# A routing table's buffers move under another expert weight slot, and two weight loads move with them

## What is computed

```python
x = x + merged(rms_norm(x)) @ w_out          # mixer: spatial gating + RG-LRU, sigmoid-gated
xf = rms_norm(x, norm2)
g_idx = argmax of 4 groups;  e_idx = top 2 of the group's 8 experts
h = silu(xf @ w_gate[e]) * (xf @ w_up[e])    # 32 experts: [1024, 256] each
x = x + sum over the 2 experts of gate * (h @ w_down[e])
y = rms_norm(x, norm_f)
```

## The kernel before

| bytes | slot | what stands there earlier |
|---|---|---|
| 0 to 48 | wslot00, wslot01 | v; free long before stage O |
| 48 to 72 | wslot20 | xh, xl |
| 72 to 96 | wslot21 | 72 to 80: wh2, wl2, used until the last unit of stage O; 80 to 97: zT, free before stage O |
| 98 to 122 | wslot10 | mh, ml, used until the last unit of stage O |
| 122 to 146 | wslot11 | ml until 130, raw from 130 to 146; from 138 on the routing tables (R_T), while they are used |

## Time and profile before

### The profile page before, as it was taken

The page is one execution under the profiler, slowest core; times in us unless marked ns, Lnnn a source line. Parts: engine busy times, 40 slices in busy tenths (PEclk is TensorE's granted clock), DMA queues, the critical chain, the costliest instruction groups (busy, mean ns, idle before and its releaser), DMA issues.

```text
span 646.4 us, 8845 instructions
## 1 busy us (share of the span) xinstructions
PE 597.8 (92%) x2860; PEld 357.3 (55%) x2860; DVE 322.9 (50%) x672; ACT 229.1 (35%) x393; POOL 53.1 (8%) x126
## 2 busy tenths in 40 slices
PE   6899999999999999999999978999999988997794
PEld 3676697877777777777568633433333333332321
DVE  4834698867767677685666764111111112111058
ACT  5414335474664746647264311111111111110124
POOL 1200001000000000000000021112121221111000
PEclk9899999999999999999999978999999999999995
DMA  8421316831222322221597489999999999999993
GB/s 306 157 95 66 114 49 228 342 104 67 73 73 97 97 74 73 73 98 55 198 396 310 179 338 369 418 421 420 419 420 420 421 419 421 418 420 420 414 317 138
DMA packets 33448, 160.61 MB, mean 248 GB/s; under 512 B 6320, under 2 KB 6704, under 8 KB 21008
## 3 DMA queue, kind: packets, MB, share of 16 engines
q1 hardware_dynamic: 27808, 149.52, 58.8%
q0 software_dynamic: 5472, 10.63, 4.5%
q10 hardware_dynamic: 144, 0.15, 0.1%
HBM read 155.01 MB, written 14.17 MB: 262 GB/s over the span
## 4 chain that ended last, share of the span: by engine, by line
PE 60%; SPq 13%; DVE 10%; DMA 10%; ACT 3%; issue 3%; ACTq 0%; DVEq 0%; POOLq 0%
PE ps L1486 12%; PE ps L1488 12%; PE ps L1487 12%; SPq L537 11%; PE ps L1829 8%; PE ps L1855 5%; DMA wslot<-in_wmoe 5%; PE ps L1605 2%; PE ps L1637 2%; DMA gy<-ytok 2%; DVE wl L908 1%; DMA ytok<-yo,idx 1%; PE ps L1691 1%; DMA raw<-in_wmix 1%; PE ps L1589 1%
## 5 line engine op out<-in xcount | busy, mean ns | idle before, releaser
L1829 PE MATMUL ps<-wslot,xgT 128*64 128x512 f32 x528 | 121.7, 594 | 11.4 <-DMA wslot<-in_wmoe 10.0
L699 ACT ACTIVATE wh<-raw 128x1024 fp32r<-128x1024 f32 x56 | 59.1, 1058 | 151.4 <-PE ps L1488 135.1
L1486 PE MATMUL ps<-xh,wh 128*128 128x512 f32 x256 | 102.5, 400 | 0.0
L1488 PE MATMUL ps<-xl,wh 128*128 128x512 f32 x256 | 100.0, 390 | 0.0
L1487 PE MATMUL ps<-xh,wl 128*128 128x512 f32 x256 | 99.9, 390 | 0.0
L908 DVE TENSOR_TENSOR wl<-raw,wh 128x1024 fp32r<-128x1024 f32 x56 | 68.5, 1223 | 46.7 <-ACT wh L699 45.6
L1829 PEld LDWEIGHTS ps<-wslot,xgT 128*64 128x64 f32 x528 | 40.0, 137 | 88.3 <-issue 86.5
L1855 PE MATMUL ps<-wslot,hT 128*64 128x512 f32 x264 | 63.8, 613 | 8.4 <-ACT hT L869 7.6
L1402 DVE SCALAR_TENSOR_TENSOR hm<-ps,rt,hs 128x256 f32<-128x256 f32 x12 | 5.8, 483 | 122.3 <-ACT hs L867 122.3
L1486 PEld LDWEIGHTS ps<-xh,wh 128*128 128x128 f32 x256 | 48.1, 188 | 16.1 <-issue 6.7
L1488 PEld LDWEIGHTS ps<-xl,wh 128*128 128x128 f32 x256 | 48.1, 188 | 10.6
(11 more groups left out here) (331 smaller groups left out, 796.0 us busy)
## 6 DMA issues: line engine op xcount, KB each, us to landing
wslot<-in_wmoe SPq DMA_DIRECT2D x97, 1024.0 KB, 21.4
raw<-in_wmix SPq DMA_DIRECT2D x56, 512.0 KB, 4.1
gy<-ytok SPq DMA_DIRECT2D x8, 512.0 KB, 8.7
xt<-in_x SPq DMA_DIRECT2D x4, 512.0 KB, 7.0
x<-in_x SPq DMA_DIRECT2D x4, 512.0 KB, 4.7
xnd<-x SPq DMA_DIRECT2D x4, 512.0 KB, 7.8
wslot<-in_wmoe SPq DMA_DIRECT2D x4, 512.0 KB, 27.3
out_y<-yf SPq DMA_DIRECT2D x4, 512.0 KB, 2.7
```

What stands on the lines that cost most here:

```text
L699: a.activation(WH[hslot], raw[:, slot, :, :].rearrange("p k c -> p (k c)"), ACT.Copy).then_inc(hi_ready, 1)
L1486: pe.matmul(out, sh, mh_, start=start, stop=False)
L1488: return pe.matmul(out, sh, ml_, start=False, stop=stop)
L1829: l = pe.matmul(ps[CAP * s:CAP * s + CAP, 2, :], xgT[:, c, CAP * s:CAP * s + CAP], wslot[q][s][:, c * 512:(c + 1) * 512], start=c == 0, st ...
```

## The change

1. The routing tables (R_T) move from 138 KB (under wslot11, part 2) to 80 KB (under wslot21, parts 1 and 2), into the memory of zT, which is free by then. `junk2` moves to 88 KB, into the same slot.
2. With that the gap of 1 KB that junk2 needed behind zT is closed: R_M, R_W, R_V, yf, wslot10, wslot11 and the small tensors lie 1 KB lower. rkx, chk, bx, posx and dgs get memory of their own.
3. The order on SP follows. Parts 1 and 2 of expert 5 are no longer issued in stage O. All three parts of expert 5 now stand behind the wait for `rt_mm`, and part 2 of expert 3 stands ahead of that wait. The stores of GROUP_A's rows (`row_out`) stand in the loop, at its last turn, which is the same place.

PE, DVE, ACT and POOL execute the same instructions in the same order as before.

```diff
-             for q, first in enumerate((0, 98, 48))]
+             for q, first in enumerate((0, 97, 48))]
...
-    R_V = 162 * K
+    R_V = 161 * K
...
-    R_M = 98 * K
+    R_M = 97 * K
...
-    R_W = 130 * K
+    R_W = 129 * K
...
-    R_T = R_W + 8 * K
+    R_T = 80 * K
...
-    junk2 = at("junk2", 96 * K, [P, 512])
-    yf = at("yf", 122 * K, [P, TILES, D])
+    junk2 = at("junk2", R_T + 8 * K, [P, 512])
+    yf = at("yf", 121 * K, [P, TILES, D])
...
-    (rkx, chk, bx, posx) = [at(n, upper_at + 256 + i * 64, [P, T2]) for i, n in enumerate(("rkx", "chk", "bx", "posx"))]
+    (rkx, chk, bx, posx) = [small(n, [P, T2]) for n in ("rkx", "chk", "bx", "posx")]
...
-    dgs = at("dgs", upper_at, [S, 2, S])
+    dgs = small("dgs", [S, 2, S])
...
             for n in range(48, STEPS):
                 step_in(n)
-                if n % 2 and n < 54:
-                    expert_part(2, 0, 4, (n - 49) // 2)
-            expert_part(2, 1, 5, 1)
-            expert_part(2, 1, 5, 2)
-            for p in range(*GROUP_A):
-                row_out(p, 4 + p)
+                if n % 2:
+                    if n < 54:
+                        expert_part(2, 0, 4, (n - 49) // 2)
+                    else:
+                        for p in range(*GROUP_A):
+                            row_out(p, 4 + p)
             row_out(3, 9)
             row_out(4, 10)
             e.wait_ge(unit_done, STEPS)
...
             e.wait_ge(xg_in, 16)
             expert_part(1, 1, 3, 1)
+            expert_part(1, 1, 3, 2)
             e.wait_ge(rt_mm, 1)
-            expert_part(1, 1, 3, 2)
-            expert_part(2, 1, 5, 0)
+            expert(2, 1, 5)
```

More of the change, by code:

```diff
@@ L173, in build @@
     hT = at("hT", R_E + 14 * K, [P, 2, P])
-    top = [182 * K]
+    top = [181 * K]
     def small(name, shape, dt=F32):
@@ L187, in build @@
     ones = small("ones", [P, P], F32)
-    upper_at = top[0]
     upper = small("upper", [P, P], F32)
```

## The result

The changed kernel takes 653.44 us (median of 9 runs) beside 649.15 us for the kernel before in the same series: a ratio of 1.007, 95% interval 1.0052 to 1.009, so +3.4 to +5.8 us. One of the nine executions on each side was far slower (865.06 us at a granted clock of 0.648, and 1197.18 us) and counts in these medians; without it they are 652.81 and 649.02 us, 3.8 us apart, and the ratio is worked out without such executions. A second series gives 1.0066 (1.0040 to 1.0091). The prediction was 652.5 us in a range of 650.4 to 654.4, slower. Its profiled execution lasts 652.5 us with a span of 650.9 us, 4.5 us more than before.

A forecast was written before the change was run, and what follows sets the result against it. The prediction took the DMA stream's bytes from 383 us on to set the end: 4.99 us for two later loads less 1.4 us given back makes 3.6 us, added to the 648.89 us median for 652.5 us, range 650.4 to 654.4.

The forecast's parts named there:

- What bounds: From 383 us on the DMA stream's bytes and idle time set the end; before that PE does, while stage O ends.
- Worth 0 in stage O: Taking parts 1 and 2 of expert 5 out of stage O empties the stream some 5 us earlier, worth 0.
- The wait for rt_mm: On SP behind the first gather, now holding expert 5 alone; already open for 2.3 us, so worth 0.
- Two loads more, 4.99 us: Five loads instead of three behind 380.33 us: 2.10 MB more at 420 GB/s delay later loads by up to 4.99 us.
- What is given back, 1.4 us: The longer queue fills the stream's hole between 400 and 403 us: 1.2 us by share, 1.6 by bytes, 1.4 taken.
- the term by SP's bytes: At 400 to 403 us SP's queue q1 could have moved 0.68 MB more, giving back 1.6 us.
- the lower bound of 2.4: Bounds 4.99 and 3.4 us; 2.4 if about 1 us idle share between 380 and 383 us is filled too.
- a sign of being wrong: Wrong if stages up to 380 us differ beyond some tenths, the hole remains or another shows, or PE awaits expert 5.
- The hole unfilled: Rival: the stream stumbles at 400 to 403 us for another reason, nothing is given back; about +5.0 us, 653.9; chance 0.14.
- PE taking the delay up: Rival: the end hangs on PE's own work, later landings only turn slack into waiting; 0, 648.9 us; chance 0.07.
- A faster stage O: Rival: fewer SBUF writes between 339 and 351 us speed PE's matmuls in stage O; faster, about 648 us; chance 0.04.
- Half absorbed: Rival: other small holes hidden in long stretches give some more back; +1.3 to +2.6 us; chance 0.07.

The follow-up runs named there:

- one load late: Kernel before, with only part 2 of expert 5 issued behind the first gather instead of in stage O: 650.19 us, +0.9, ratio 1.0020.
- the changed kernel with the gap used: Changed kernel, with parts 0 and 2 of expert 2 issued before stage O ends, three loads left behind the first gather: 648.82 us beside 647.95.
- third late load: Kernel before, with parts 1 and 2 of expert 5 and part 2 of expert 4 issued late: 655.93 us, +6.7, ratio 1.0101.
- the first experiment: Kernel before with all its addresses, only parts 1 and 2 of expert 5 issued late (two loads late): 652.09 us beside 649.27, ratio 1.0052.
- The repeated profile: The changed kernel run and profiled once more, nothing altered, beside the kernel before: 653.78 us beside 649.27, +4.5.
- The two that use the gap: Changed kernel and kernel before, each with parts 0 and 2 of expert 2 issued before stage O ends: 648.82 and 649.30 us beside 647.95.

## Why the prediction was right

- *What bounds.* Right. The stream is full behind the gather, the tail is unchanged (52.1 against 51.9 us), and PE's waits for weights took the delay up only as waiting (14.6 us; 13.5 was forecast).
- *Worth 0 in stage O.* Right. The stream runs empty by about 346 us. Three profiles without these loads and without the dip had the first gather 0.5 to 1.0 us earlier than before (375.65, 375.39 and 375.85 against 376.36), but they were ahead by as much at SP's last loads of `raw` at 335 us, where their programs do not differ yet. From there to the router's product (line 1691), in the kernel before and with one load late:

```profile
335.98 2.85 SPq L489 DMA_DIRECT2D raw<-in_wmix  x2
...
358.99 1.87 PE L1691 MATMUL ps<-wrt,xn2T 128*128 128x36 f32 x16
```
```profile
335.05 2.83 SPq L489 DMA_DIRECT2D raw<-in_wmix  x2
...
358.02 1.87 PE L1691 MATMUL ps<-wrt,xn2T 128*128 128x36 f32 x16
```

  That is 23.01 and 22.97 us, and 22.99 and 22.97 us in the two others (two loads late, and the changed kernel with the gap used). In the changed kernel it is 24.43 us (335.07 to 359.50): the dip costs 1.4 us.
- *The wait for rt_mm.* Right: 378.5 us (377.16 + 1.36) against 381.57, open 3 us before SP comes to it.
- *Two loads more, 4.99 us.* Right in kind and size: the second and third late load cost 2.3 to 2.5 us each, where 2.50 was worked out. So the rate of 420 GB/s was the one to take, and not a lower one. The prediction calls it the rate of HBM reads, which reads too much into it: it is all that the engines moved, scatters included, and the queue with the weights (q1) moved 72.91 MB in those 191 us, 382 GB/s.
- *What is given back, 1.4 us.* Right in kind, too small. Against 4.99 us the changed kernel's distance grew by 3.06 and 2.92, and 2.85 in the first experiment, so 1.9 to 2.1 us come back; one late load gives 1.94. The traces say where. Taking what each stretch moved less than 420 GB/s as time lost, the kernel before loses 1.6 us in the first 3 us behind SP's resumption, 0.2 us from there to 400 us, and 1.7 us from 400 to 404 us (246 GB/s); the changed kernel loses the same 1.6 us, then nothing (423 GB/s up to 400 us, 418 to 404). So the hole itself gives 1.6 us, which is the term by SP's bytes and not the middle that I took, and some 0.3 us come from smaller gaps ahead of 400 us. The idle share between 380 and 383 us, the reason for the lower bound of 2.4, gave nothing.
- *What I left out, and luck.* Behind SP's resumption the shift is +3.0 us, not +3.6. The median came out above the forecast (+4.3), and the profiles show time lost ahead of SP's resumption as well. In the first SP resumes 1.24 us later: 0.75 us by a slower first gather, and 0.5 us by its later start, which is 1.4 us of clock dip less the 0.9 us by which this execution was ahead at 335 us. Why the gather is slower in it isn't shown. The repeated profile has the dip (2.6 us up to the gather's start) and not the slow gather. So two misses of opposite sign stand behind the fit of the total; at equal clock it is +3.64. The prediction had named as a sign of being wrong that the stages up to 380 us are not the same to some tenths. In both profiles of the changed kernel they are not, by 1.2 and 2.6 us. Nothing shows that the change makes this, but the sum has no term for it.
- *Rivals.* The hole unfilled is out (share 1.01 there). PE taking the delay up is out: the third late load costs its full price. A faster stage O is out, by the 23.0 us above; the argument that the prediction held against it, that PE is busy 5.00 of 5 us, would not have told, since a slowed PE is busy as well. Half absorbed had the right idea of other small gaps, but the +3.0 us behind the gather lie within the bounds of the sum.

No version beat the kernel before. The two that use the gap tie with it. What would have to shorten is the way from the end of stage O to the first pass, which decides when the refills start; that wasn't tried.

## What to carry to other kernels

Where a transfer stream is full to the end, look for the last moment at which it stands empty: bytes moved ahead of it are free, each behind it costs its time at the stream's rate. The price is not linear: the first bytes fill the holes behind that moment (here 2 us of them), and taking more bytes away than are needed to keep the stream full bought nothing that showed here. When memory is overlaid, choose what a late-living buffer lies under by which load it holds back, and count how many loads stand on each side of the gap.

## What was unexpected

- One gather of 128 rows of 4 KB took 3.7 to 4.8 us (eight profiles, from POOL's issue to SP's release) where the loads ahead of it had all but landed, and 7.98 us with two more 1 MB loads queued (one profile): beside bulk loads it took about twice as long, and PE waited for it.
- Executions of one kernel differ by up to 5 us (646.9 to 652.1 us for before in the first series) with the mean granted clock (0.969 to 0.981). A dip between 340 and 350 us, under matmuls that run without a break, came in five profiles of nine; what starts it the traces did not show.
